# Where four kinds of background steps stand in the order of a transformer block's matmul halves

## The chip, the cores and the metric

The kernel runs on one core of a Trainium2 chip. The metric is the device time of one execution in microseconds, the median of several runs. Engines are named TensorE (PE), VectorE (DVE), ScalarE (ACT), GpSimd (POOL) and SyncE (SP).

## What is computed

Two blocks run one after the other on 256 tokens of width 2048, in float32. The part that the change touches is the first block:

```python
mod = c_act @ w_ada[l] + b_ada[l]
sh_a, sc_a, gt_a, sh_f, sc_f, gt_f = [m[:, None, :] for m in jnp.split(mod, 6, axis=-1)]
h = _rmsnorm(x, norm_mix[l]) * (1.0 + sc_a) + sh_a
p = h @ w_in[l]
c_q, c_kv, k_pe, q_g, k_g, v_g, z, b_logit, a_logit, gate_logits = _split_cols(p)
y_a = _mla_branch(...) @ w_o_mla[l]
y_b = _gdn_branch(...) @ w_o_gdn[l]
g_a, g_b = jnp.split(jax.nn.sigmoid(gate_logits), 2, axis=-1)
mix = (g_a * y_a + g_b * y_b) @ w_o[l]
x = x + gt_a * mix
h = _rmsnorm(x, norm_ffn[l]) * (1.0 + sc_f) + sh_f
gate, up = jnp.split(h @ w_gate_up[l], 2, axis=-1)
x = x + gt_f * ((jax.nn.silu(gate) * up) @ w_down[l])
```

`w_ada` is 2048 by 12288: the product of one row `c_act` with it gives six vectors of 2048. The second block is a gated MLP with a spatial product over the tokens.

## The kernel before

**Halves.** Every matrix product is a Job: 512 columns of a weight, taken in units of four k-tiles (1 MiB, one load). A unit is split in two halves of two k-tiles. ScalarE casts a half to a high part (line 1456), VectorE subtracts it from the raw weight for the low part (line 1904), and TensorE multiplies high by high, low by high and high by low in one-pass float32 (lines 1179 to 1181 with the tokens as rows of the result, 24 shorter matmuls at lines 1191 to 1193 for the jobs with side "ch", conv among them). Weights land in a ring of three raw buffers and are split into four places; the split of a half needs a place that TensorE has done with, and so runs up to four halves ahead.

**The order.** `Schedule` writes one list of steps out by hand rules, and every engine's program takes its own part of that list, in the list's order. Between halves runs `slot()`: each generator in the background list `bg` advances once, in the order in which they joined. A yield is therefore a half of delay, wherever nothing else slows it. `consume` first stages splits (and loads) as far as places are free, then emits the half.

**Modulation.** The products with `w_ada` are made on VectorE (line 1885) with the columns of the weight scaled by `c_act` and summed in GA, 24 chunks of 512 columns in four units each. Chunks 0 to 7 are made in the front; the 64 units of chunks 8 to 23 are put between the weight units by `plan_units`: behind every second unit, behind each one in conv 3 and 4, never in ga 2 (and for chunks from 20 on, never in wo 3 and gate 0). Two buffers of GA serve in turn; `ga_busy` tells that one still waits for its sum to be used. When the first unit of a chunk finds it busy, `stage_next` runs forced slots until it is free. The sum over two parts (`ga_sum`, line 1891) is followed by matmuls over the partitions: for chunks 8 to 15 `mod` (line 1133), which waits for a slot in which a job has 2 to 5 steps left, and for chunks 16 to 23 `gt` (line 1315), one per gate row. The gate row is added to its bias in GT on VectorE (line 2235). The bias comes by one load, put by `gate_bias`. `gt` always uses bank 7.

**Mix.** In og, VectorE forms the gated sum with four instructions per job (lines 2212 and 2215). `to_hl` then has TensorE transpose it in two groups (line 1100, banks 4, 5, 6, 7 in turn over all such groups), ScalarE copies the high part and VectorE makes the low one (line 2225). A user of a bank first waits for its last reader:

```python
            n = 4 + (num - 1) % 4
            take(n)
```

**Turns.** Behind wo, down and the last product, the rows are normalized and transposed again. `turn_chunk` puts the squares of a finished column part (ScalarE, line 1656) behind the addition to the residual (VectorE, lines 2253 and 2255); `run_blocks` runs the last product of each tile by tile.

The halves around the change have these numbers: conv 4 is 70 to 77, conv 5 78 to 85, gb 3 174 to 181, og 0 to og 3 182 to 197 in fours, wo 0 198 to 205, wo 2 214 to 221, wo 3 222 to 229.

Of the kernel before, what the change touches and what calls it, by code (L numbers as in the profile page):

```python
# [319 lines left out]
class Schedule:  # L320
# [30 lines left out]
    def plan_units(self, jobs, extra):  # L351
        u = self.units
        u.extend(("g", ci, q) for ci in range(2) for q in range(4))
        for c in range(4):
            f = [("g", 2 * c + 2 + i // 4, i % 4) for i in range(8)] if c < 3 else []
            w = [("w", j, 4 * c, 4) for j in jobs[:4]]
            u.extend([w[0]] + f[:1] + [w[1]] + f[1:5] + [w[2]] + f[5:] + [w[3]])
        self.start_units = len(u)
        order = [(j, t0) for j in jobs[4:] for t0 in range(0, j.nkt, j.step)]
        p = [i for i, (j, _) in enumerate(order) if j.name == "wout" and j.c in ((3, 0), (3, 1))]  # L360
        order[p[1]], order[p[2]] = order[p[2]], order[p[1]]
        for k, (j, t0) in enumerate(order):
            u.append(("w", j, t0, min(j.step, j.nkt - t0)))
            never = (("ga", 2),) if extra and extra[0][1] < 20 else (("wo", 3), ("gate", 0))
            if extra and (k % 2 or j.name == "conv" and j.c in (3, 4)) and (j.name, j.c) not in never:
                u.append(extra.pop(0))

    def raw_slot(self, i):
# [62 lines left out]
    def mod_reduce(self, ci):  # L431
        for n in range(4):
            if n == 2:
                self.put("ga_sum", ci)
            yield
        q = 1 - self.current
        while self.pending[q] in self.bg or (not 2 <= self.left <= min(5, self.total - 2) and not self.forced):
            yield
            q = 1 - self.current
        self.put("mod", ci, q)  # L440
        self.put("mod_e", ci, q)
        self.ga_busy[ci % 2] = False
        self.have.add(("mod", ci))
        yield
# [422 lines left out]
                self.have.add(("ogdn", tt, g))  # L867

    def to_hl(self, kind, c):
        yield  # L870
        yield
        for g in range(2):
            self.hl_n += 1
            self.put("hl", kind, c, g, self.hl_n)
            self.hl_of[(kind, c, g)] = self.hl_n
            self.have.add(("hl", kind, c, g))
            yield

    def gate_row(self, ci):

        name = "gta" if ci < 20 else "gtf"
        for n in range(4):
            if n == 2:
                self.put("ga_sum", ci)
            yield
        while (name, "bias") not in self.have:
            yield
        self.put("gt", name, ci % 4, ci)
        self.ga_busy[ci % 2] = False
        self.have.add((name, ci % 4))  # L890
        yield

    def gate_bias(self, name):
        self.put("gate_bias", name)
        for _ in range(3):
            yield
        self.have.add((name, "bias"))

    def turn_chunk(self, n, c):
        self.put("turn_sq", n, c, (0, 1))  # L900
        yield

# [1764 lines left out]
```

## Time and profile before

| What | Value |
|---|---|
| Median of 3 runs | 2312.42 us (2311.53 to 2314.65) |
| The profiled execution | 2316.55 us, span 2315.3 us |
| TensorE busy | 2250.3 us, 97% of the span |
| VectorE, ScalarE, GpSimd busy | 65%, 44%, 1% |
| DMA | 506.75 MB, 219 GB/s over the span |
| Mean granted TensorE clock | 0.992 |

The profiled execution's span runs from its first to its last instruction; what lies around it is 1.25 us. Matmuls overlap in the records, so a row's duration is longer than the step from its start to the next one's. A wait is named by the instruction that ended it.

### The profile page before, as it was taken

Reading aid. Unit: us, or ns where it says so; the run is one execution under the profiler, and the core shown is the slowest. Engines: PE = TensorE matmul, PEld = TensorE weight load, DVE = VectorE, ACT = ScalarE, POOL = GpSimd, SP = SyncE. Lnnn points to the kernel's source line nnn. Section 1 sums busy time; section 2 is a strip of 40 time slices with the busy share of each in tenths; the row PEclk is TensorE's granted clock in tenths of the full one; section 3 lists DMA queues with packets and bytes.
Section 4 is the critical chain, followed back from the end, with each engine's and each line's share of the span. In section 5 each row is a group of like instructions: output and inputs, shape, how many; then the busy total and the mean of one; then the engine's idle time right before and its main releaser. Section 6 shows DMA issues by size and latency. Waiting matters only on the chain.

```text
span 2315.3 us, 26964 instructions
## 1 busy us (share of the span) xinstructions
PE 2250.3 (97%) x10799; PEld 1863.7 (80%) x10799; DVE 1500.3 (65%) x1878; ACT 1017.4 (44%) x1282; POOL 23.6 (1%) x28
## 2 busy tenths in 40 slices
PE   5999999999998999999999999999999999999998
PEld 3688898888886878888888888887888888888886
DVE  5888888787767767765554455566555555555555
ACT  4355444433443464443344434446444444444344
POOL 0000000000000000000000000000000000000000
PEclk9999999999999999999999999999999999999999
DMA  9966767576687758875555555554565556555553
GB/s 363 382 242 206 232 218 245 196 264 208 212 293 252 273 202 300 280 259 193 196 188 182 200 189 193 185 203 174 193 200 186 187 189 198 182 190 187 193 191 134
DMA packets 276445, 506.75 MB, mean 219 GB/s; under 512 B 24032, under 2 KB 38112, under 8 KB 275296
## 3 DMA queue, kind: packets, MB, share of 16 engines
q1 hardware_dynamic: 276320, 505.03, 64.1%
q8 instruction: 85, 1.39, 0.2%
q14 instruction: 40, 0.33, 0.0%
HBM read 502.51 MB, written 2.49 MB: 218 GB/s over the span
## 4 chain that ended last, share of the span: by engine, by line
PE 81%; DVE 8%; DMA 5%; issue 3%; ACT 3%; SPq 1%; POOL 0%; DVEq 0%; ACTq 0%
PE bank L1179 24%; PE bank L1180 24%; PE bank L1181 24%; DVE WL L1904 3%; DMA RAW<-in_w_o_dram 2%; PE bank L1367 2%; PE bank L1100 1%; ACT WH L1456 1%; DVE GA L1885 1%; DMA RAW<-in_w_in_dram 1%; DVE A L2118 1%; PE bank L1191 1%; PE bank L1192 1%; PE bank L1193 1%; PE bank L1127 1%
## 5 line engine op out<-in xcount | busy, mean ns | idle before, releaser
L1904 DVE TENSOR_TENSOR WL<-RAW,WH 128x1024 fp32r<-128x1024 f32 (+1 forms) x714 | 864.8, 1218 | 618.5 <-ACT WH L1456 614.6
L1456 ACT CAST WH<-RAW 128x1024 fp32r<-128x1024 f32 (+1 forms) x714 | 743.1, 1047 | 915.7 <-PE bank L1181 744.7
L1179 PE MATMUL bank<-WH,HTh 128*128 128x512 f32 x1936 | 769.8, 398 | 2.9 <-DVE WL L1904 2.9
L1181 PE MATMUL bank<-WH,HTl 128*128 128x512 f32 x1936 | 755.2, 390 | 0.0
L1180 PE MATMUL bank<-WL,HTh 128*128 128x512 f32 x1936 | 755.1, 390 | 0.0
L1179 PEld LDWEIGHTS bank<-WH,HTh 128*128 128x128 f32 x1936 | 364.3, 188 | 82.4 <-DVE WL L1904 5.2
L1180 PEld LDWEIGHTS bank<-WL,HTh 128*128 128x128 f32 x1936 | 364.5, 188 | 77.6 <-issue 4.6
L1181 PEld LDWEIGHTS bank<-WH,HTl 128*128 128x128 f32 x1936 | 364.1, 188 | 76.8
L1885 DVE SCALAR_TENSOR_TENSOR GA<-RAW,ST,GA 128x512 f32<-128x512 f32 x264 | 181.2, 746 | 12.9 <-DMA RAW<-in_w_ada_dram 7.7
L1179 PE MATMUL bank<-WH,R2h 128*128 128x512 f32 x408 | 165.0, 405 | 3.0 <-DVE WL L1904 3.0
L1180 PE MATMUL bank<-WL,R2h 128*128 128x512 f32 x408 | 160.3, 393 | 0.0
L1181 PE MATMUL bank<-WH,R2l 128*128 128x512 f32 x408 | 160.1, 392 | 0.0
L1179 PE MATMUL bank<-WH,aTh 128*128 128x512 f32 x344 | 134.2, 390 | 1.1 <-DVE WL L1904 1.1
L1181 PE MATMUL bank<-WH,aTl 128*128 128x512 f32 x344 | 133.9, 389 | 0.0
L1180 PE MATMUL bank<-WL,aTh 128*128 128x512 f32 x344 | 133.9, 389 | 0.0
L1191 PE MATMUL bank<-HTh,WH 128*128 128x256 f32 x384 | 113.2, 295 | 3.2 <-DVE WL L1904 3.1
L1192 PE MATMUL bank<-HTl,WH 128*128 128x256 f32 x384 | 109.7, 286 | 0.0
L1193 PE MATMUL bank<-HTh,WL 128*128 128x256 f32 x384 | 109.6, 285 | 0.0
L1179 PEld LDWEIGHTS bank<-WH,R2h 128*128 128x128 f32 x408 | 77.5, 190 | 21.3 <-DVE WL L1904 3.8
L1180 PEld LDWEIGHTS bank<-WL,R2h 128*128 128x128 f32 x408 | 77.5, 190 | 17.5 <-issue 2.0
L1181 PEld LDWEIGHTS bank<-WH,R2l 128*128 128x128 f32 x408 | 77.4, 190 | 16.6
L1191 PEld LDWEIGHTS bank<-HTh,WH 128*128 128x128 f32 x384 | 74.7, 195 | 5.4 <-DVE WL L1904 4.7
(271 smaller groups left out, 1771.8 us busy)
## 6 DMA issues: line engine op xcount, KB each, us to landing
RAW<-in_a_w_in_dram SPq DMA_DIRECT2D x96, 1024.0 KB, 5.0
RAW<-in_w_gate_up_dram SPq DMA_DIRECT2D x88, 1024.0 KB, 5.0
RAW<-in_w_ada_dram SPq DMA_DIRECT2D x80, 1024.0 KB, 5.2
RAW<-in_w_in_dram SPq DMA_DIRECT2D x63, 1024.0 KB, 5.0
RAW<-in_w_down_dram SPq DMA_DIRECT2D x44, 1024.0 KB, 5.0
RAW<-in_a_w_out_dram SPq DMA_DIRECT2D x32, 1024.0 KB, 5.0
A<-in_w_ada_dram SPq DMA_DIRECT2D x16, 1024.0 KB, 11.7
RAW<-in_w_o_dram SPq DMA_DIRECT2D x16, 1024.0 KB, 5.4
```

The lines of the kernel that those rows point to most:

```text
L1100: t = e.transpose(dst[:, i * P:(i + 1) * P], s, ident)
L1127: i = e.matmul(b, L.CB[:, t, :], rv[:, t, :], start=False, stop=t == 3)
L1179: e.matmul(o, ah[:, s], hi[:, k, :], start=first, stop=False)
L1180: e.matmul(o, ah[:, s], lo[:, k, :], start=False, stop=False)
L1181: i = e.matmul(o, al[:, s], hi[:, k, :], start=False, stop=last)
L1191: e.matmul(o, hi[:, k, s], ah, start=first and cb % 2 == 0, stop=False, skip_group_check=True)
L1192: e.matmul(o, hi[:, k, s], al, start=False, stop=False, skip_group_check=True)
L1193: i = e.matmul(o, lo[:, k, s], ah, start=False, stop=last, skip_group_check=True)
L1367: i = e.matmul(dst[:, h, :], left[:, h, :], right[:, h, :], start=True, stop=True)
L1456: e.copy(hi, rv).then_inc(S["hi"], 1)
L1885: e.scalar_tensor_tensor(out=g, in0=rv[:, t, :], scalar=col, in1=g, op0=ALU.mult, op1=ALU.add).then_inc(S["ga_dve"], 1)
L1904: e.tensor_tensor(lo, rv, hi.bitcast(F32), ALU.subtract).then_inc(S["lo"], 1)
```

## The change

The bias counts as there after eight yields instead of three. A gate row waits until the row before it is marked there, which is two yields behind its own step; formerly each waited for the bias alone. `mod_reduce` yields twice more before it looks for a slot for the mod matmuls. `to_hl` yields three times instead of twice for the mix. `turn_chunk` yields once before the squares of column part 2 of the first two turns. In `plan_units` gb 3 gets no w_ada units, and og 2 and og 3 get one behind each of their units.

```diff
+        thick = (("conv", 3), ("conv", 4), ("og", 2), ("og", 3))
         for k, (j, t0) in enumerate(order):
             u.append(("w", j, t0, min(j.step, j.nkt - t0)))
-            never = (("ga", 2),) if extra and extra[0][1] < 20 else (("wo", 3), ("gate", 0))
-            if extra and (k % 2 or j.name == "conv" and j.c in (3, 4)) and (j.name, j.c) not in never:
+            never = (("ga", 2), ("gb", 3)) if extra and extra[0][1] < 20 else (("wo", 3), ("gate", 0))
+            if extra and (k % 2 or (j.name, j.c) in thick) and (j.name, j.c) not in never:
                 u.append(extra.pop(0))
...
             if n == 2:
                 self.put("ga_sum", ci)
             yield
+        yield
+        yield
         q = 1 - self.current
...
     def to_hl(self, kind, c):
-        yield
-        yield
+        for _ in range(3 if kind == "mix" else 2):
+            yield
...
-        while (name, "bias") not in self.have:
+        before = (name, "bias" if ci % 4 == 0 else ci % 4 - 1)
+        while before not in self.have:
             yield
         self.put("gt", name, ci % 4, ci)
         self.ga_busy[ci % 2] = False
+        for _ in range(2):
+            yield
         self.have.add((name, ci % 4))
-        yield
 
     def gate_bias(self, name):
         self.put("gate_bias", name)
-        for _ in range(3):
+        for _ in range(8):
             yield
         self.have.add((name, "bias"))
 
     def turn_chunk(self, n, c):
+        if c == 2 and n < 5:
+            yield
         self.put("turn_sq", n, c, (0, 1))
         yield
```

## Rows read from the trace of the kernel before

**Rows 1.** Page, part 1: busy us, share of the span, instructions
```profile
PE 2250.3 (97%) x10799; PEld 1863.7 (80%) x10799; DVE 1500.3 (65%) x1878; ACT 1017.4 (44%) x1282; POOL 23.6 (1%) x28
```

**Rows 2.** Who waited for whom, TensorE: us in total, times, longest
```profile
PE bank L1179 <- DVE WL L1904: 6.9, 8, 2.7
PE bank L1315 <- DVE A L2235: 6.7, 1, 6.7
...
PE bank L1133 <- DVE GA L1891: 3.7, 1, 3.7
...
PE bank L1100 <- DVE A L2215: 1.7, 1, 1.7
```

**Rows 3.** Windows (PE, PEld, DVE, ACT, POOL busy; clock, DMA share, GB/s); timeline
```profile
354.79:361.62 6.83, 6.83 (x34) 6.83 (x34) 5.53 (x7) 0.78 (x2) 0.00 (x0) 0.50 0.74 249
...
849.72:853.13 3.41, 3.41 (x14) 2.93 (x13) 0.64 (x2) 3.24 (x9) 0.00 (x0) 0.50 1.04 392
...
849.44 1.74 PE L1100 MATMUL bank<-CST,A 128*128 128x128 f32 x8 [1.89 <-DVE A L2292]
```

**Rows 4.** Timeline, TensorE, behind half 81: start us, us, instruction
```profile
350.43 0.28 PE L1193 MATMUL bank<-HTh,WL 128*128 128x256 f32 x1
354.44 1.58 PE L1133 MATMUL bank<-CST,GA 128*128 128x1 f32 x8 [3.73 <-DVE GA L1891]
```

**Rows 5.** Timeline, VectorE, at the same place
```profile
351.36 1.22 DVE L1904 TENSOR_TENSOR WL<-RAW,WH 128x1024 fp32r<-128x1024 f32 x1
...
353.70 0.69 DVE L1891 TENSOR_TENSOR GA<-GA 128x512 f32<-128x512 f32 x1
```

**Rows 6.** Timeline, TensorE, gate rows 0 and 1
```profile
695.72 1.02 PE L1315 MATMUL bank<-GA,CST 128*128 128x512 f32 x2
703.47 2.05 PE L1315 MATMUL bank<-GA,CST 128*128 128x512 f32 x2 [6.73 <-DVE A L2235]
704.53 1.42 PE L1179 MATMUL bank<-WH,R2h 128*128 128x512 f32 x1
```

**Rows 7.** Timeline, VectorE, the same two rows
```profile
702.63 0.69 DVE L2235 TENSOR_TENSOR A<-bank,A 128x512 f32<-128x512 f32 x1 [7.05 <-DMA A<-in_b_ada_dram]
705.56 0.69 DVE L2235 TENSOR_TENSOR A<-bank,A 128x512 f32<-128x512 f32 x1 [2.23 <-PE bank L1315]
```

**Rows 8.** Timeline, TensorE, gate row 2
```profile
757.84 1.02 PE L1315 MATMUL bank<-GA,CST 128*128 128x512 f32 x2
...
758.94 0.40 PE L1180 MATMUL bank<-WL,HTh 128*128 128x512 f32 x1
```

**Rows 9.** Timeline, VectorE, in og 1 and og 2
```profile
719.11 2.73 DVE L1885 SCALAR_TENSOR_TENSOR GA<-RAW,ST,GA 128x512 f32<-128x512 f32 x4
...
722.89 0.68 DVE L2212 SCALAR_TENSOR_TENSOR A<-A,bank 128x512 f32<-128x512 f32 x1
...
725.54 2.35 DVE L1904 TENSOR_TENSOR WL<-RAW,WH 128x1024 fp32r<-128x1024 f32 x2
727.81 0.68 DVE L2225 SCALAR_TENSOR_TENSOR HTl<-bank,HTh 128x512 fp32r<-128x512 f32 x1
```

**Rows 10.** Timeline, TensorE and VectorE, first mix transposes
```profile
714.39 0.48 PE L1179 MATMUL bank<-WH,R2h 128*128 128x512 f32 x1
...
715.30 0.69 DVE L2225 SCALAR_TENSOR_TENSOR HTl<-bank,HTh 128x512 fp32r<-128x512 f32 x1 [1.04 <-ACT HTh L1643]
```

**Rows 11.** Timeline, SyncE and ScalarE, a load of wo 0; page of loads, median to landing
```profile
752.50 3.83 SPq L2536 DMA_DIRECT2D RAW<-in_w_o_dram x2
...
757.52 2.00 ACT L1456 CAST WH<-RAW 128x1024 fp32r<-128x1024 f32 x2 [0.43 <-DMA RAW<-in_w_o_dram]
...
A<-in_x_dram SPq DMA_DIRECT2D x4, 1024.0 KB, 8.2
```

**Rows 12.** Timeline, TensorE and VectorE, last splits of wo 3 and down
```profile
824.96 0.50 PE L1179 MATMUL bank<-WH,HTh 128*128 128x512 f32 x1 [1.23 <-DVE WL L1904]
...
823.68 1.23 DVE L1904 TENSOR_TENSOR WL<-RAW,WH 128x1024 fp32r<-128x1024 f32 x1 [1.73 <-ACT WH L1456]
...
1568.83 0.50 PE L1179 MATMUL bank<-WH,aTh 128*128 128x512 f32 x1 [1.05 <-DVE WL L1904]
```

## What the change is expected to do

> **What bounds the kernel now.** I read the page first: TensorE is busy for 97% of the span, VectorE 65% [rows 1]. So only what lets TensorE run earlier can pay, and the question is where its idle time lies. The list of who waited for whom [rows 2] has few entries behind the opening: 6.7 us once for a VectorE instruction of line 2235, 3.7 us once for line 1891, 6.9 us in eight pieces for the low halves (line 1904), and 1.7 us once for line 2215. I then looked at each on the timeline. A matmul is shown as 0.39 us long, but in a dense run they start 0.23 us apart, so I take losses from start to start.
>
> The clock counts too. Behind the 3.7 us wait the granted clock is 0.50 (the 1.2 GHz level) for 6.83 us, all of them busy, and behind an idle time of 1.89 us it is 0.50 for 3.41 us [rows 3]. A busy stretch at half clock does half the work, so a long wait costs 1.7 or 3.4 us more; the 1.7 us wait of line 2215 had no such stretch. I call it a dip and take 2.3 us as its mean, an estimate between these two.
>
> I number the matmul halves as the schedule does ("half 182" is the first of og 0); a token-side half is 12 matmuls, 2.72 us. A background generator advances once per slot, and there is one slot behind each half.
>
> **A. Sum of chunk 11 in conv 5.** The mod matmuls of chunk 11 stand behind half 81. The last matmul before them starts at 350.43, they start at 354.44, after the sum (line 1891, 353.70 to 354.39) [rows 4, 5]. The change puts two more slots between the sum and the matmuls. Half 83 still has two halves left of its job, so the window for mod (2 to 5 left) is met there and mod 11 moves exactly two halves on. The sum is then no wait. What is late next: half 82 needs its own low half, which VectorE makes from 351.36 to 352.58 [rows 5] in an order that the change leaves as it is. TensorE is free at 350.6, so it now waits 2.1 us there, where it waited 3.9. That gives 1.8 us. The dip behind the old wait cost 3.4 us (6.83 us at 0.50) [rows 3]. Whether a 2.1 us wait still brings one is open: 1.89 us did, 1.7 us did not. With chance 0.6 for a dip of 2.3 us, A gives 5.2 − 1.4 = 3.8 us, between 1.8 and 5.2. The other modulation chunks: 9, 10, 14 and 15 move by two halves, 8, 12 and 13 not at all (they wait for the window or are forced); no wait of TensorE hangs on them, and I count 0, with 0.5 us either way.
>
> **B. Gate rows.** Now gate rows 0 and 1 are issued in one slot before half 185, and both use bank 7: the second waits until VectorE has added the first to its bias, and the bias lands only at 702.6 [rows 6, 7]. From the first row (695.72) to half 185 (704.53) are 8.8 us, and half 185 itself takes 1.3 us too long, in the half-clock stretch. A gate row that waits for nothing costs 0.87 us (757.84 to 758.94, less one matmul step) [rows 8]. So the place costs 8.8 + 1.3 − 1.7 = 8.4 us. In the change the bias counts as there eight slots on. Counted: its generator starts behind half 182 and ends in the slot behind 190; the unit (18, 0) is staged before half 191, finds its buffer busy and forces one slot, in which row 0 goes out; row 1 follows two halves on, behind half 192. TensorE reaches row 0 near 712.8, 10 us after the bias landed. The 8.4 us are gone. The mix transposes move one half on, and that clears the 1.7 us wait of line 2215 too (with the restart 1.8): 10.2 us in all.
>
> But two waits come in their place, both in bank 7. The eight mix transposes take banks 4, 5, 6, 7 in turn, so numbers 4 and 8 use bank 7. Number 4, formerly clear of the rows, goes out behind half 192; row 1 goes out in the same slot and ahead of it (its generator joined the list earlier). Number 8 moves from behind half 200 to behind half 201, into the slot of row 2, again behind it. Each time TensorE stands until VectorE has added that row, and VectorE works in order: all its queued work is in front.
>
> Row 1: from the low half of transposes 1 or 2 to the addition VectorE has an ada (2.65 us), three more splits (1.15 each), one combine of og (2.65), two mix low halves and a sum (0.61 each), an ada of two (1.33), one split more and rows 0 and 1 (0.61 each) [rows 9]: 14.3 us, against 13.3 us of TensorE's (four halves, two transposes of 0.44, two rows). It starts 1.6 us behind TensorE as between 714.39 and 715.99 [rows 10], or 0.8 us more if the load for half 190 still queues behind x and the bias. So it ends row 1 by 1.0 plus 1.6 to 2.4 us behind TensorE's matmuls of it. Stall 2.6 to 3.4; I take 3.3.
>
> Row 2: between the two stalls stand the thick units, an ada behind each load of og 2 and og 3: from the end of the first stall VectorE has three adas, one combine, a mix low half and five splits up to the combine of og 3, 17.0 us, begun 1.8 us late (transposes, ScalarE's copy), and a load that comes about 0.9 us late; TensorE has two transposes and five halves, 14.5 us. So VectorE starts that combine 5.2 us late. Combine, low half and split are 4.4 us, TensorE's next three halves and two transposes 9.0 us: it waits 0.9 us for the low half of half 201 with the signals. Behind that low half hangs the load of the last wo 0 unit (three buffers in turn): such a load was issued at 752.50 and used by ScalarE at 757.52 [rows 11], 5.0 us; then come a cast (1.0), the split (1.2) and the row (0.7). From the low half to row 2 these are, with the signals, 8.1 us; TensorE has half 201 and the row, 3.6 us. Stall 4.5 us (in the kernel before TensorE was 2.6 us further behind, and nobody else needed bank 7). With the dip behind it 2.3 us; a dip behind row 1 is swallowed, as VectorE and the loads set the time of row 2. Where the other costs go: two ada units leave gb 3, with two loads of SyncE's queue and 5.3 us of VectorE; TensorE waited for nothing there, so that gives nothing. The bias load keeps its place in SyncE's queue, GpSimd's queue has none of the moved steps. Costs: 3.3 + 0.9 + 4.5 + 2.3 = 11.0, of which some 0.8 are the transposes' starts that I counted twice: 10.2. B is 10.2 − 10.2 = 0, between −3 and +4.
>
> Can the loads keep up? The thick stretch wants two loads of 1 MiB per two halves, 2.1 MB in 5.44 us, 385 GB/s; the profile has a stretch with 392 GB/s at full DMA share [rows 3]. I count no more for it. The Trainium skill, HBM Reference, Specifications, gives about 358 GB/s as a core's share of its memory domain, though more for a core that streams alone; by the share the eight loads would take an estimated 1.7 us longer than TensorE's 21.8 us and B would be −1.7. The trace speaks for the lone core's figure.
>
> **C. Squares behind the last split.** TensorE waits for the low half of half 229 (1.23 us shown, 1.4 from start to start; line 1904 from 823.68) and in down for its counterpart (1.05 shown, 1.2) [rows 12]. ScalarE cast that half only after two squares that wait for the residual sums. One slot on, the cast comes first; VectorE does the split straight behind the residual, at about 823.1, before TensorE's 823.6. Both waits go: 2.6 us, with 0.4 us of slack at the first. The squares are needed only for the norm after the next tile. The later waits of the turns (as at 849.44) keep their distance to the tile and stay. The gate rows of the second bias come long after it: 0.
>
> **Sum.** 3.8 + 0 + 2.6 = 6.4 us. The profiled execution took 2316.55 us (span 2315.3), so it would take 2310.2; it lies 4.1 us above the median of 2312.42, and the median becomes 2306.0. About 0.2%, 4.6 us, is what a measurement of this kernel can tell from no change.
>
> **The rivals.** (1) *As forecast*, chance 0.52: 2302 to 2309. (2) *The clash in bank 7 costs next to nothing*, if VectorE is ahead there: B is 10.2 less 1.3 per row at most, so A, B and C give 14 to 17 us, 2297. For it: VectorE is only 65% busy [rows 1]; against: the count above. Chance 0.13. (3) *B eats the rest*: a dip at A, both dips in B and loads a little late, B −4, A 1.8: 2312. Chance 0.27. (4) *Slower*: the three-buffer ring in the thick stretch. A buffer is loaded again only after its landing and use; the landing took 5.0 us here, but 8.2 us for x, which shared the queues [rows 11]. With 8.2 each of four rounds of the ring grows by 3 us, 12 us in all, less the 6.4: 2318. It decides from 2.8 us per load on. Chance 0.08.
>
> Range for 8 in 10: 2298 to 2312. Faster by over 0.2% are (2) and most of (1): 0.62; within: 0.30; slower: 0.08.
>
> **What would show it.** Before half 185 no gap; one row before half 191, one behind 192. TensorE's transposes waiting for line 2235 twice, about 3 and 4.5 us; no wait for line 1891, but about 2 us for line 1904 near 350; no gap at 823 and 1567. Wrong if line 2235 shows under 1 us in all (then 2297), or over 12 us or ScalarE waits for loads of og 2 and og 3 above 3 us each (then no gain).

## The result and the profile after

The changed kernel takes 2307.56 us (median of 11 runs, 2306.18 to 2309.81), the kernel before 2312.62 us in the 11 runs beside them (2307.88 to 2317.45). The ratio is 0.9979, interval 0.9969 to 0.9988: faster by 5.1 us. The interval, 0.12 to 0.31%, is clear of no change but lies on both sides of the 0.2% that the prediction took as its bound. The forecast was 2306.0.

The profiled execution has a span of 2305.0 us, 10.3 less than the one of before. That pair of traces flatters the change, and where is seen below. Lines are seven higher than in the rows of before: line 2242 was 2235, 1911 was 1904, 1892 and 1898 were 1885 and 1891, 1107 was 1100, 1186 to 1188 were 1179 to 1181, 1322 was 1315, 2222 was 2215, and 2303 was 2296.

The page, busy time by engine, and who waited for whom (TensorE's rows: us in total, times, longest):

```profile
PE 2245.4 (97%) x10799; PEld 1860.5 (81%) x10799; DVE 1499.3 (65%) x1878; ACT 1016.1 (44%) x1282; POOL 23.5 (1%) x28
...
PE bank L1107 <- DVE A L2242: 7.6, 2, 4.1
...
PE bank L1198 <- DVE WL L1911: 4.1, 4, 1.9
...
PE bank L1186 <- DVE WL L1911: 3.1, 7, 1.1
...
PE bank L1107 <- DVE A L2299: 1.9, 1, 1.9
...
PE bank L1107 <- DVE A L2303: 1.5, 1, 1.5
...
PE bank L1107 <- DVE A L2222: 0.5, 1, 0.5
```

Against [rows 2]: the 6.7 us of the second gate row and the 3.7 us of the mod sum are gone, and the 1.7 us for a combine of og (its four-instruction gated sum) are down to 0.5. New are two entries. Twice, 7.6 us in all, the mix transposes wait for the addition of a gate row to its bias. And once, 1.5 us, transposes behind down wait for line 2303, which nobody had forecast; it costs no time, as the last section shows. The waits for low halves at line 1186 went from 6.9 to 3.1 us; 2.3 of that are part C's, and 2.4 come from one at 226 us, where the change reaches nothing (the last section comes back to it).

**Part A, behind half 81.** Timeline, TensorE, and VectorE:

```profile
349.31 0.39 PE L1198 MATMUL bank<-HTh,WH 128*128 128x256 f32 x1 [1.30 <-DVE WL L1911]
...
348.05 1.21 DVE L1911 TENSOR_TENSOR WL<-RAW,WH 128x1024 fp32r<-128x1024 f32 x1
...
350.38 0.68 DVE L1898 TENSOR_TENSOR GA<-GA 128x512 f32<-128x512 f32 x1
...
347.00:355.00 8.00, 6.70 (x56) 6.49 (x54) 8.00 (x12) 2.95 (x3) 0.07 (x1) 1.00 0.41 137
```

The sum (350.38) now comes after half 82 has begun and holds nobody; half 82 waits for its own low half. The last row, a window, has the granted clock as its third number from the end: 1.00, where [rows 3] have 0.50 for 6.83 us. Aligned by the starts of the halves, halves 82 to 84 take 5.6 us less than before.

**Part B, og 1 to wo 0.** Timeline, TensorE, at gate rows 1 and 2, then the two windows of half clock:

```profile
711.93 1.02 PE L1322 MATMUL bank<-GA,CST 128*128 128x512 f32 x2
716.39 0.65 PE L1107 MATMUL bank<-CST,A 128*128 128x128 f32 x4 [3.45 <-DVE A L2242]
...
744.86 1.02 PE L1322 MATMUL bank<-GA,CST 128*128 128x512 f32 x2
750.00 1.11 PE L1107 MATMUL bank<-CST,A 128*128 128x128 f32 x4 [4.12 <-DVE A L2242]
...
717.83:721.24 3.41, 3.41 (x10) 2.67 (x9) 3.41 (x6) 1.06 (x1) 0.00 (x0) 0.50 0.72 263
748.55:755.38 6.83, 5.38 (x15) 4.42 (x16) 3.31 (x4) 1.53 (x2) 0.00 (x0) 0.50 0.56 204
```

A row that holds nobody costs 0.87 us [rows 8]; row 1 takes 4.46 us and row 2 5.14, so the two clashes cost 3.6 and 4.3 us. VectorE's timeline says why the wait is that long. Around row 1:

```profile
710.26 0.68 DVE L2242 TENSOR_TENSOR A<-bank,A 128x512 f32<-128x512 f32 x1
710.86 0.68 DVE L1898 TENSOR_TENSOR GA<-GA 128x512 f32<-128x512 f32 x1
711.46 1.41 DVE L1892 SCALAR_TENSOR_TENSOR GA<-RAW,ST,GA 128x512 f32<-128x512 f32 x2
712.79 1.22 DVE L1911 TENSOR_TENSOR WL<-RAW,WH 128x1024 fp32r<-128x1024 f32 x1
713.92 0.68 DVE L2232 SCALAR_TENSOR_TENSOR HTl<-bank,HTh 128x512 fp32r<-128x512 f32 x1
714.52 1.21 DVE L1911 TENSOR_TENSOR WL<-RAW,WH 128x1024 fp32r<-128x1024 f32 x1
715.65 0.68 DVE L2242 TENSOR_TENSOR A<-bank,A 128x512 f32<-128x512 f32 x1
```

The last line is the addition that reads bank 7. TensorE had the row ready at 712.9, but VectorE was only then beginning a split (712.79), and behind it stood a low half of the mix (713.92) and another split (714.52): three instructions, 2.8 us, and then the addition's own 0.7. The Trainium skill, TensorE: Matmul & The Clock Gate, the table at its head, says that VectorE works its queue strictly first in, first out; this trace agrees: the addition, which could have run from 712.9, starts at 715.65, in its place. Around row 2 VectorE waits too; ScalarE's cast, SyncE's load and VectorE's split and addition:

```profile
741.98 0.37 SPq L2543 DMA_DIRECT2D RAW<-in_w_o_dram  x1
...
746.95 1.04 ACT L1463 CAST WH<-RAW 128x1024 fp32r<-128x1024 f32 x1 [3.22 <-DMA RAW<-in_w_o_dram]
...
748.12 1.22 DVE L1911 TENSOR_TENSOR WL<-RAW,WH 128x1024 fp32r<-128x1024 f32 x1 [1.37 <-ACT WH L1463]
749.26 0.68 DVE L2242 TENSOR_TENSOR A<-bank,A 128x512 f32<-128x512 f32 x1
```

The chain is the forecast one: load 5.0 us (741.98 to 746.95), cast 1.0, split, addition.

**Part C.** Timeline, ScalarE and VectorE, at the end of wo 3; the cast (810.15) comes before the square (813.91), and TensorE waits for no low half there, nor in down:

```profile
810.15 2.00 ACT L1463 CAST WH<-RAW 128x1024 fp32r<-128x1024 f32 x2 [0.80 <-DMA RAW<-in_w_o_dram]
813.91 0.63 ACT L1663 ACTIVATE A<-A 128x512 f32<-128x512 f32 x1 [1.76 <-DVE A L2262]
...
815.12 1.22 DVE L1911 TENSOR_TENSOR WL<-RAW,WH 128x1024 fp32r<-128x1024 f32 x1
```

**Where the 10.3 us of this pair of traces come from:** 2.6 us lie before half 81 and 1.6 at gate 0, where the change reaches nothing; there the two executions differ in their stretches of half clock and in the wait at 226. A gave 5.6, B cost 2.9 (from half 184 to half 203), C gave 1.4 and 1.2. That makes 5.3 us of the change's own (5.6 − 2.9 + 2.6), with the medians 5.1 us apart; the rest, 0.8 us of the 10.3, is spread. That the two agree so well is in part chance: the half-clock stretch that A removed was 6.83 us in this trace of the kernel before and in e2's, but 3.41 in e3's.

### The profile page after: what moved, and what is told of

The parts are those of the page before. It is cut to its first block, busy times and chain, and to the rows that moved or that the text cites. A ratio compares the mean times of both kernels' runs of the same rounds, so it can differ in the third digit from the quotient of the medians.

```text
span 2305.0 us, 26967 instructions
## 1 busy us (share of the span) xinstructions
PE 2245.4 (97%) x10799; PEld 1860.5 (81%) x10799; DVE 1499.3 (65%) x1878; ACT 1016.1 (44%) x1282; POOL 23.5 (1%) x28
## 4 chain that ended last, share of the span: by engine, by line
PE 85%; DVE 7%; DMA 3%; ACT 2%; issue 2%; SPq 1%; POOL 0%; DVEq 0%; ACTq 0%
PE bank L1186 25%; PE bank L1188 25%; PE bank L1187 25%; DVE WL L1911 2%; PE bank L1374 2%; PE bank L1107 1%; DVE GA L1892 1%; PE bank L1198 1%; ACT WH L1463 1%; PE bank L1200 1%; PE bank L1199 1%; DVE A L2125 1%; DMA RAW<-in_w_o_gdn_dram 1%; PE bank L1134 1%; PE bank L1346 1%
## 5 line engine op out<-in xcount | busy, mean ns | idle before, releaser
L1892 DVE SCALAR_TENSOR_TENSOR GA<-RAW,ST,GA 128x512 f32<-128x512 f32 x264 | 181.1, 745 | 12.9 <-DMA RAW<-in_w_ada_dram 7.7
```

Source lines behind the costliest of these rows:

```text
L1892: e.scalar_tensor_tensor(out=g, in0=rv[:, t, :], scalar=col, in1=g, op0=ALU.mult, op1=ALU.add).then_inc(S["ga_dve"], 1)
```

## The experiments

All were timed in five rounds beside the kernel before; ratios are to that kernel on the same chip. The microseconds by which a run is called faster or slower are worked out from the ratio; for the three single parts the medians alone give 2.6 faster (e1), 3.3 slower (e2) and 3.5 faster (e3).

### The three parts alone

**e1_sum_only**, the kernel before with part A alone:

```diff
+        yield
+        yield
         q = 1 - self.current
```

> The kernel before with the two more yields between a modulation sum and its matmuls alone. Theory (the parts add up as costed): the 3.9 us wait for line 1891 near 350 becomes about 2 us for a low half, its stretch at half clock goes; 3.5 to 5.5 us faster than the kernel before. Rival (VectorE is the bound in conv 5, so the wait is only shifted): the low halves of 83 to 86 take the time back, under 1.5 us faster.

Measured: 2310.28 us against 2312.88, ratio 0.9984 (0.9975 to 0.9993), 3.7 us faster. TensorE's wait at half 82, and the window behind it (lines are two higher than before):

```profile
353.63 0.39 PE L1193 MATMUL bank<-HTh,WH 128*128 128x256 f32 x1 [1.93 <-DVE WL L1906]
...
355.00:362.00 7.00, 7.00 (x61) 6.99 (x60) 6.25 (x7) 1.66 (x3) 0.00 (x0) 1.00 0.63 201
```

The low half is what comes late next, as forecast, and no stretch of half clock follows. None does at this place in any of the eight traces of kernels with part A.

**e2_rows_and_mix_only**, the changed kernel without A and C (the `thick` units, the gate rows and bias, and `to_hl` as in the change).

> The kernel before with the bias, the chained gate rows, the placement of the w_ada units and the later mix transposes, without the two yields behind the sums and without the later squares. Theory: the 8.4 us at half 185 and the 1.7 us wait for the mix go, and two waits in bank 7 of about 3.6 and 4.3 us with their stretches at half clock come, so 1 us faster to 4 us slower than the kernel before. Rival (this part carries the gain, the other two are within noise): 4 us or more faster.

Measured: 2316.2 us, ratio 1.0009 (1.0 to 1.0018), 2.1 us slower, with no difference at the edge of the interval. Who waited for whom, TensorE:

```profile
PE bank L1103 <- DVE A L2238: 7.7, 2, 4.2
...
PE bank L1136 <- DVE GA L1894: 3.6, 1, 3.6
```

The two waits in bank 7 are there in full and the wait of conv 5, which this kernel keeps, too. So the largest part of the edit gains nothing; a theory by which it carries the gain falls.

**e3_squares_only**, the kernel before with part C alone:

```diff
     def turn_chunk(self, n, c):
+        if c == 2 and n < 5:
+            yield
```

> The kernel before with the squares of column part 2 one slot later alone. Theory: two waits of 1.4 and 1.2 us go, no other appears, 2.6 us faster, between 2 and 4. Rival (the wait moves to the transposes of the next turn): no change, and the waits for lines 2292 and 2296 longer by as much.

Measured: 2309.41 us, ratio 0.9983 (0.9974 to 0.9992), 3.9 us faster. The forecast 2.6 us lie within the interval (1.9 to 6.0). On its trace the wait in down is gone, the one at the end of wo 3 only in part: against the trace of the kernel before the two places give 1.2 and 0.4 us, so that more than half of the 3.9 us is not seen there. The rival's longer wait does appear, 1.5 us for the counterpart of line 2296, but in the place of a half-clock stretch, and it takes nothing back (last section). TensorE there, and ScalarE's cast of that unit:

```profile
820.26 0.50 PE L1181 MATMUL bank<-WH,HTh 128*128 128x512 f32 x1 [0.84 <-DVE WL L1906]
...
814.00 2.00 ACT L1458 CAST WH<-RAW 128x1024 fp32r<-128x1024 f32 x2 [2.01 <-DMA RAW<-in_w_o_dram]
```

The cast does come before the squares; but the load was late (2.01 us of waiting, 0.80 in the changed kernel). With it came late the first of the two splits, and behind that, as in the changed kernel too, the residual and then the second split, for which TensorE waits. So the gain of this place hangs on the load too; in the changed kernel and in e9 the wait is gone.

**e9_sum_and_squares**, A and C together, without B.

> The kernel before with the two yields behind the sums and the later squares, without the part on gate rows, units and mix. Theory (the parts add up and the third one loses time): the gains of the two parts, 0.16% and 0.17% by their own runs, add up to 6 to 8 us, so it is 1 to 3 us faster than the changed kernel, near 2305. Rival (the parts only pay together, or the two gains overlap): 0.2% or less against the kernel before, the same as the changed kernel.

Measured: 2304.22 us against 2312.14, ratio 0.9966 (0.9952 to 0.998), 7.9 us faster. A and C add up (3.7 + 3.9 = 7.6), and by the ratios this kernel is some 3 us faster than the changed one (0.9966 against 0.9979), though the two intervals overlap. The kernel keeps the 7.0 us wait for the gate rows.

### The bank of the gate rows

**e4_rows_in_bank_4**, the changed kernel with the four gate rows of the first bias in bank 4:

```diff
-            take(7)
-            e.matmul(bank[7], ones, L.GA[:, ci % 2, 0, :], start=True, stop=True).then_inc(S["mod_t"], 1)
-            held[7] = [("gt", ci - 15)]
+            n = 4 if name == "gta" else 7
+            take(n)
+            e.matmul(bank[n], ones, L.GA[:, ci % 2, 0, :], start=True, stop=True).then_inc(S["mod_t"], 1)
+            held[n] = [("gt", ci - 15)]
...
-            e.tensor_tensor(row, bank[7], row, ALU.add).then_inc(S["gt"], 1)
+            e.tensor_tensor(row, bank[4 if name == "gta" else 7], row, ALU.add).then_inc(S["gt"], 1)
```

> The changed kernel with the first four gate rows in bank 4 instead of bank 7; order and work are the same. Theory (the two new waits are the bank's, not VectorE's speed): both waits for the addition of a row go, 7.6 us, with the half-clock stretches behind them; some 1.5 to 3 us come back as waits for low halves in og 3 and wo 0, because VectorE and the loads are late there; 5 to 9 us faster than the changed kernel, about 2300. Rival (VectorE's queue in the thick stretch is the bound and the bank only shows it): the waits turn into waits for low halves of the same length, within 1.5 us of the changed kernel, about 2307.

Measured: 2300.21 us, ratio 0.9944 (0.993 to 0.9958), 12.9 us faster than before and about 8.1 faster than the changed kernel. Timeline, TensorE, behind the same two rows and at the places where it waits instead (lines one higher than after):

```profile
712.21 1.02 PE L1323 MATMUL bank<-GA,CST 128*128 128x512 f32 x2
713.07 0.60 PE L1107 MATMUL bank<-CST,A 128*128 128x128 f32 x4
...
728.64 0.50 PE L1186 MATMUL bank<-WH,HTh 128*128 128x512 f32 x1 [0.32 <-DVE WL L1912]
...
736.18 0.50 PE L1186 MATMUL bank<-WH,HTh 128*128 128x512 f32 x1 [1.76 <-DVE WL L1912]
...
740.56 0.50 PE L1186 MATMUL bank<-WH,HTh 128*128 128x512 f32 x1 [0.90 <-DVE WL L1912]
...
743.42 1.02 PE L1323 MATMUL bank<-GA,CST 128*128 128x512 f32 x2
744.28 0.60 PE L1107 MATMUL bank<-CST,A 128*128 128x128 f32 x4
```

Behind each row the transposes start 0.86 us on, with no wait: both clashes are gone. They had cost 3.6 + 4.3, with some 4.35 us of half clock behind them, 12.2 us in all. TensorE does not get the whole of it: it now waits three times for low halves, 3.6 us from start to start (728.64: 0.6, 736.18: 1.9, 740.56: 1.1). The 8.1 us measured, uncertain by some 4, fit what is left, 8.6. No stretch of half clock is shown between 700 and 760.

**e5_row_2_in_bank_4**, the same with row 2 alone in bank 4 (`name == "gta" and c == 2`).

> The changed kernel with only gate row 2 in bank 4; rows 0, 1 and 3 stay in bank 7. Theory (two separate clashes): the wait of 3.6 us at half 193 stays with its half-clock stretch, the one of 4.3 us at half 202 goes; 4 to 6 us faster than the changed kernel, some 2 us slower than with all rows in bank 4, about 2302.5. Rival (one backlog of VectorE seen twice): with the first wait still there VectorE catches up, and freeing the second gives all that freeing both gives, about 2300.

Measured: 2302.41 us against 2310.52, ratio 0.9959 (0.9946 to 0.9971). One wait in bank 7 is left, row 1's:

```profile
PE bank L1107 <- DVE A L2243: 3.5, 1, 3.5
```

The two clashes are separate: row 1's stays at its old size when row 2's goes. A stretch of half clock follows it here too (at 718.16). It is the trace that shows this: of the times, 0.9959 against e4's 0.9944, the intervals overlap, and they alone would not refute the rival.

### The half of delay for the mix

**e7_mix_as_before**, the changed kernel with `for _ in range(2):` in `to_hl` for all kinds; the rows stay in bank 7.

> The changed kernel with the mix transposes after two yields as before. Then they stand one half ahead of the gate rows, and rows 1 and 2 wait for the low half of transposes 4 and 8 in bank 7. Theory: the order within the bank turns round but VectorE's backlog stays, so TensorE waits about 2 us at rows 1 and 2 each and about 2 us each for the combines of og 1 and og 3; within 3 us of the changed kernel. Rival (the half of delay itself makes the clash, without it the gain of the rows comes free): 5 us or more faster than the changed kernel, near 2301.

Measured: 2302.09 us, ratio 0.9962 (0.9948 to 0.9976). My theory had this kernel within 3 us of the changed one, and it is 8.8 us faster than before instead of 5, some 4 faster than the changed one by the ratios: less than the rival's 5 as well, so the time decides little. The trace does. Who waited for whom, and the longest wait on the timeline:

```profile
PE bank L1107 <- DVE A L2222: 5.4, 3, 2.4
...
738.47 0.90 PE L1107 MATMUL bank<-CST,A 128*128 128x128 f32 x3 [2.36 <-DVE A L2222]
```

No wait for line 2242 is left, and rows 1 and 2 wait for nothing, though my theory had them wait 2 us each. So the rival had the mechanism right: it is the third yield of `to_hl` that puts transposes 4 and 8 right behind rows 1 and 2. With two yields they go out ahead of the rows, and TensorE waits three times for the combines of og instead, which is cheaper.

**e8_mix_as_before_bank_4**, both edits: rows in bank 4 and two yields.

> The mix transposes after two yields as before, and the first four gate rows in bank 4. Theory (the later mix saves only waits for the combines): TensorE waits about 2 us at transposes 3 and 7 for line 2222's counterpart, no wait in a bank; 2 to 4 us slower than rows in bank 4 with the later mix, about 2303. Rival (the mix delay is worth nothing once the bank is free): 2300.

Measured: 2301.02 us, ratio 0.9956 (0.9944 to 0.9969). TensorE waits three times for the combines, 4.9 us in all, longest 1.9. By the ratios that is 2.8 us slower than e4, within the 2 to 4 expected, but the uncertainty of the difference is some 4 us: what the third yield is worth once the bank is free stays open.

### The place of the units

**e6_rows_in_4_units_in_wo0**, e4 with the closely set w_ada units (one behind each weight unit) in wo 0 instead of og 2 and og 3:

```diff
-        thick = (("conv", 3), ("conv", 4), ("og", 2), ("og", 3))
+        thick = (("conv", 3), ("conv", 4), ("wo", 0))
```

> All first four gate rows in bank 4, and the w_ada units that the change crowds into og 2 and og 3 crowd into wo 0 instead, where VectorE has no combine of og. Theory (what is left there are low halves late behind the crowded units and combines): the 3.5 us of low-half waits in og 3 and wo 0 shrink to under 1.5, 1 to 3 us faster than rows in bank 4 alone, about 2298. Rival (the loads are the bound, two per two halves wherever they stand): the waits move into wo 0 and the time stays at 2300.

Measured: 2304.8 us, ratio 0.997 (0.9959 to 0.9982): some 6 us slower than e4 by the ratios, so the theory that the crowding is cheaper in wo 0 falls. It does cost time in og 2 and og 3: by the start of half 202 this kernel is 4.8 us ahead of e4. But it costs more in wo 0 and behind it: by half 217, in wo 2, this kernel is 4.1 us behind. The largest single loss is a low half in wo 1, with 3.41 us of half clock behind it. Timeline, ScalarE and TensorE:

```profile
756.79 1.05 ACT L1464 CAST WH<-RAW 128x1024 fp32r<-128x1024 f32 x1 [5.49 <-DMA RAW<-in_w_o_dram]
...
764.86 0.50 PE L1186 MATMUL bank<-WH,HTh 128*128 128x512 f32 x1 [2.57 <-DVE WL L1912]
```

ScalarE waits 5.49 us for a load, and the low half is 2.57 us late. The rival (loads) is the closer one, though its 2300 was missed by 4.8 us; and gate row 2, the first residual and the squares stand in front of the casts there too; which of them sets the 2.57 us was not tried.

## Why the forecast came out

**Part A: right.** The sum was forecast to cost nothing in its new place and the low half to come late by 2.1 us; it waits 1.30 us after and 1.93 in e1. The 3.8 us contained a chance of 0.6 for a dip of 2.3 us; none came in either trace, so A gave 5.6 us in the pair, while timed alone it gave 3.7 (1.6 to 5.8). The place and the order are shown; the size is right within the interval. As the stretch behind the old wait was 3.41 us in one trace and 6.83 in two, the 3.4 us counted for it were the high end.

**Part B: the waits right, the clock term too small.** Rows 0 and 1 cost 8.81 us and half 185 another 1.34; less two rows at 0.87 that is 8.4 us gained, as forecast. The combine's wait gave 1.9 (forecast 1.8). Of the costs, the clashes were forecast at 3.3 and 4.5 and measured 3.6 and 4.3, and instead of 0.9 us for the low half of half 201 there are two small waits of 0.6 and 0.4 at other places. What failed is the sentence "a dip behind row 1 is swallowed". The trace has two dips, and neither is: starts of matmuls behind row 1 lie 1.6 us further apart in sum than at full clock, behind row 2 2.75 us, 4.35 against the 2.3 counted. Nor was there anything to match the 0.8 us that I took off for transposes counted twice. So the costs were 3.6 + 4.3 + 4.35 + 1.0 = 13.2 and not 10.2, and B is −10.3 + 13.2 = +2.9 us (forecast 0, range −3 to +4), with +2.1 measured in e2 and about +3 between e9 and the changed kernel.

**Part C: right.** 1.4 and 1.2 us at the two places, forecast 1.4 and 1.2; alone 3.9 (1.9 to 6.0), though e3's trace shows that the first of the two needs the load in time, and shows only 1.6 us at the two places. The 0.4 us of slack that I gave it was the right warning. The later waits of the turns were to stay, and at the second turn one of 1.46 us is new; that it costs nothing was not foreseen (last section).

**The sum.** −3.7, +2.1 and −3.9 multiply to a ratio of 0.9976 against the measured 0.9979: no interaction is seen, and with each part uncertain by 2 us none under some 4 us would be. The 1.5 us between 2306.0 and 2307.56 can be read as B's missing 3 us, in part made up by A and C, which alone came out at 7.6 instead of 6.4; that two misses of opposite sign brought the forecast so close is luck.

**The rivals.** Rival 2 (the clash costs nothing, 2297) is refuted by the 7.6 us of waits; e4 shows what it would have been, 2300.2. Rival 3 (B eats the rest, 2312) had the direction of B right, but its loss at A did not come. Rival 4 (the ring of three buffers) did not come either: the landing that counted took 5.0 us. One sign was badly chosen: I had written that no gain would be left if ScalarE waited over 3 us each for the loads of og 2 and og 3. For loads that were issued there, the ones of wo 0's weights, it waited 3.51, 4.50 and 3.22 us, and the gain was there: ScalarE has 56% of the span idle, it waited 4.12 us for such a load in the kernel before too, and only at row 2 does such a wait hold TensorE for long. On the quarrel between the Trainium skill's share (HBM Reference, Specifications) and the lone core's rate the trace speaks for the lone core: the second of the 40 slices of the page after, 57.6 us long, has 381 GB/s, above the share. The thick stretch itself did not need so much: at its densest, 729 to 740, it had 337 GB/s at a DMA share of 0.91.

**Whose gain it is.** All of it comes from the two small edits, a yield or two each; the large one removes a 6.7 us wait, and gives the time back as two waits in bank 7, where another bank would have done.

## What to carry to other kernels

When a step is moved past other users of the same PSUM bank, count not its own duration but the whole queue in front of the instruction that reads the bank: here 0.9 us of matmul held TensorE for 4.5 and 5.1 us, and another bank number made 8 us of it vanish. A wait of TensorE is to be priced with the half-clock stretch that may follow, each wait for itself, and before one is counted as swallowed, look for what TensorE waits for next: behind rows 1 and 2 nothing was, behind down all of it was. And of an edit with several parts each should be timed alone: the part with the longest text was the one that lost.

## What was not expected of the hardware

The same wait can bring a stretch of half clock or not. At the first turn, between wo 3 and the gated product behind it, TensorE waits 1.89 us before and 1.87 after; before, the granted clock then was 0.50 for 3.41 us [rows 3]. After (timeline and window):

```profile
842.17 0.66 PE L1107 MATMUL bank<-CST,A 128*128 128x128 f32 x4 [1.87 <-DVE A L2299]
...
838.00:846.00 8.00, 6.13 (x36) 4.97 (x35) 3.63 (x7) 5.79 (x14) 0.56 (x1) 1.00 0.53 191
```

It stays at 1.00. Of the eleven traces two, this one and e4's, have no such stretch there.

A stretch can also cost nothing. Behind down, at the second turn, which leads into the second block, TensorE is idle for 2.48 us; what that idle time waits for the profile does not show. The kernel before, with the window behind it, and then the changed kernel:

```profile
1583.25 0.47 PE L1179 MATMUL bank<-R2h,HTh 128*128 128x512 f32 x1 [2.48 <-issue]
...
1591.81 1.09 PE L1100 MATMUL bank<-CST,A 128*128 128x128 f32 x8
...
1583.58:1586.99 3.41, 3.41 (x10) 2.63 (x9) 1.69 (x3) 2.60 (x7) 0.00 (x0) 0.50 0.25 95
```

```profile
1572.98 0.47 PE L1186 MATMUL bank<-R2h,HTh 128*128 128x512 f32 x1 [2.48 <-issue]
...
1581.52 1.09 PE L1107 MATMUL bank<-CST,A 128*128 128x128 f32 x8 [1.46 <-DVE A L2303]
```

Before, 3.41 us at half clock follow, and the transposes start 8.56 us on without a wait. After, no stretch follows, and they start 8.54 us on, behind a wait of 1.46 us for VectorE. VectorE sets the time there, and the stretch was swallowed. The same holds in all eleven traces: four have the stretch (before, e1, e2, e4) and no such wait, the other seven the wait and no stretch.

Such a stretch can even pay. TensorE waits 1.88 us at 199 us of the span in these kernels, and 27 us later for a low half; that second wait is 2.67 us in e1 and 2.68 in the kernel before, but 0.23 in the changed kernel, where half clock (3.41 us at 199.0) followed the first. The other traces agree: e3, e4 and e8 have half clock at 199 to 201 too, and wait 0.20, 0.35 and 1.36 us, while the seven traces without that stretch wait 2.3 to 2.7. VectorE had caught up in the longer time. The same matmul in the changed kernel and in e1:

```profile
224.86 0.50 PE L1186 MATMUL bank<-WH,R2h 128*128 128x512 f32 x1 [0.23 <-DVE WL L1911]
```

```profile
226.67 0.55 PE L1181 MATMUL bank<-WH,R2h 128*128 128x512 f32 x1 [2.67 <-DVE WL L1906]
```

In the kernel before, 6.83 us at half clock followed the second wait as well. So the changed kernel, 1.4 us behind after the first stretch, is 3.2 us ahead at 231 of the kernel before's trace, and 2.6 at half 81: that is the 2.6 us by which this pair of traces flatters the change. Nor does the length of the stretch go by the wait: the 3.45 us wait of row 1 had 3.41 us at 0.50, the 4.12 us wait of row 2 had 6.83, in e9 the second wait here, 2.56 us, had none; and one early stretch, which no part of the change touches, took 6.83 us before and 10.24 after. In e7 a wait of 2.36 us had 3.41 us at half clock, while those of 1.93 in e1 and 1.76 in e4 had none. That some of the spread of the kernel before (2307.9 to 2317.5 us) comes from this is likely: over the 27 runs of that kernel beside e1 the slower ones have the lower mean clock (correlation −0.69). It is not shown, as each run but the profiled one gives a mean clock and no stretches.
